# Attention unit 2's turn moved behind head 0's queries, unit 5's probabilities in another buffer, mix(1,a,1) ahead of tile 1's attention

## The reference

```python
proj = rms_norm(x) @ w_in                                  # u, v, q, k, v
a_out = gelu(u) * (w_s @ rms_norm(gelu(v)) + b_s)          # per block of 128 tokens, 8 groups
b_out = banded_chunk_attention(q, k, v)                    # 8 heads of 64, softmax
x = x + concat(a_out, b_out) @ w_out
q = rms_norm(x) @ w_query                                  # 8 routing heads, 2 x 128
s_top, i_top = top_k(q @ sub_keys, 16)                     # per half
best, pos = top_k(s_top[0][:, None] + s_top[1][None, :], 16)
eidx = i_top[0] * 128 + i_top[1]                           # at pos
h = gelu(expert_u[eidx] . x)
x = x + sum(softmax(best) * h * expert_v[eidx])            # 16384 experts, 16 a head and token
```

## Time and profile before

| | us |
|---|---|
| median of three runs | 1156.43 |
| the profiled execution, its own time | 1155.34 |
| its span | 1153.5 |
| TensorE matmuls busy | 1048.9 (91%) |
| VectorE busy | 769.7 (67%) |
| ScalarE busy | 568.4 (49%) |
| GpSimd busy | 289.4 (25%) |
| DMA, mean over the span | 322 GB/s |

### The profile page before, as it was taken

The page is one execution under the profiler, slowest core; times in us unless marked ns, Lnnn a source line. Parts: engine busy times, 40 slices in busy tenths (PEclk is TensorE's granted clock), DMA queues, the critical chain, the costliest instruction groups (busy, mean ns, idle before and its releaser), DMA issues.

```text
span 1153.5 us, 12038 instructions
## 1 busy us (share of the span) xinstructions
PE 1048.9 (91%) x4092; PEld 667.5 (58%) x4092; DVE 769.7 (67%) x1499; ACT 568.4 (49%) x1237; POOL 289.4 (25%) x261
## 2 busy tenths in 40 slices
PE   8999999998898779799877887789999999999998
PEld 6888464454454333344322232259878778888886
DVE  5788777667666657676676665554675496777743
ACT  7664544544443444643444345354765555444532
POOL 0001445444535325453443444400000000000000
PEclk9999999999999989999999999999999999999999
DMA  9848999999999999999999999977443454555540
GB/s 349 341 167 304 421 422 422 421 421 422 420 421 422 421 422 421 422 421 420 422 422 421 422 411 422 421 291 269 177 146 131 163 186 161 183 187 191 196 156 36
DMA packets 55532, 371.87 MB, mean 322 GB/s; under 512 B 6192, under 2 KB 7344, under 8 KB 12080
## 3 DMA queue, kind: packets, MB, share of 16 engines
q0 software_dynamic: 36864, 268.45, 56.0%
q1 hardware_dynamic: 18608, 102.65, 24.2%
HBM read 370.03 MB, written 1.05 MB: 322 GB/s over the span
## 4 chain that ended last, share of the span: by engine, by line
PE 53%; DMA 31%; DVE 7%; ACT 6%; issue 3%; POOL 0%; SPq 0%; DVEq 0%; POOLq 0%; ACTq 0%
DMA uv<-in_peer_uv,eidx 30%; PE bank L2269 14%; PE bank L1968 7%; PE bank L1970 7%; PE bank L1969 7%; PE bank L2445 6%; PE bank L2040 4%; PE bank L2444 3%; DVE uv L1581 3%; DVE w_lo L1290 1%; ACT w_hi L806 1%; ACT diag L1026 1%; PE bank L1939 1%; ACT chosen L1023 1%; PE bank L2158 1%
## 5 line engine op out<-in xcount | busy, mean ns | idle before, releaser
L2269 PE MATMUL bank<-uv,diag 128*128 128x512 f32 x1024 | 490.8, 614 | 90.9 <-ACT diag L1026 90.6
L1581 DVE SCALAR_TENSOR_TENSOR uv<-uv,xn 128x1024 f32<-128x1024 f32 x256 | 313.7, 1225 | 209.6 <-DMA uv<-in_peer_uv,eidx 209.5
L730 POOL DMA_INDIRECT uv<-in_peer_uv,eidx x256 | 289.1, 1129 | 457.3 <-PE bank L2269 329.3
L2269 PEld LDWEIGHTS bank<-uv,diag 128*128 128x128 f32 x1024 | 184.3, 193 | 362.1 <-issue 359.9
L1290 DVE TENSOR_TENSOR w_lo<-wraw,w_hi 128x2048 fp32r<-128x2048 f32 x69 | 157.7, 2290 | 94.7 <-ACT w_hi L806 94.7
L1018 ACT ACTIVATE chosen<-chosen 128x1 f32<-128x1 f32 x256 | 51.8, 202 | 327.7 <-DVE uv L1581 327.2
L806 ACT CAST w_hi<-wraw 128x2048 fp32r<-128x2048 f32 x69 | 131.6, 1909 | 124.2 <-PE bank L1970 62.1
L2445 PE MATMUL bank<-nT_both,w_hi 128*128 128x512 f32 x320 | 109.6, 396 | 0.0
L1026 ACT ACTIVATE diag<-const,chosen 128x128 f32<-128x128 f32 x256 | 102.8, 401 | 8.3
L1023 ACT ACTIVATE chosen<-chosen 128x1 f32<-128x1 f32 x256 | 75.4, 295 | 9.3
L2444 PE MATMUL bank<-nT_both,w_lo 128*128 128x256 f32 x280 | 78.1, 279 | 0.0
(11 more groups left out here) (326 smaller groups left out, 1363.4 us busy)
## 6 DMA issues: line engine op xcount, KB each, us to landing
wraw<-in_ff_in SPq DMA_DIRECT2D x22, 1024.0 KB, 4.7
wraw<-in_ff_out SPq DMA_DIRECT2D x11, 1024.0 KB, 4.7
wraw<-in_query SPq DMA_DIRECT2D x4, 1024.0 KB, 5.0
uv<-in_peer_uv,eidx POOLq DMA_INDIRECT x256, 15.0
wraw<-in_in_q SPq DMA_DIRECT2D x2, 1024.0 KB, 8.3
wraw<-in_in_k SPq DMA_DIRECT2D x2, 1024.0 KB, 9.0
wraw<-in_pool_o SPq DMA_DIRECT2D x2, 1024.0 KB, 4.7
wraw<-in_sb_o SPq DMA_DIRECT2D x2, 1024.0 KB, 4.6
```

The source lines that it names most:

```text
L730: pool.indirect_dma_start(out=uv[:, RING_AT[n % RING], :], out_offset=None, in_=io["peer_uv"], in_offset=bass.IndirectOffsetOnAxis(ap=eidx ...
L1581: nc.vector.scalar_tensor_tensor(out=u, in0=u, scalar=1.0, in1=xn[:, head // PEER_HEADS, :], op0=ALU.mult, op1=ALU.mult, accum_out=hdot[he ...
L2269: mm = nc.tensor.matmul(acc[m][:, :], diag[:, n % RING, :], uv[:, RING_AT[n % RING], D + m * HALF:D + (m + 1) * HALF], start=(n % (ROWS // ...
```

## The change

Five things are changed. Unit 2 is turned behind head 0's queries, where unit 3 was turned, and its copy on ScalarE goes behind head 0's route. Unit 3 is turned behind mix(1,a,1). mix(1,a,1) goes from behind the attention of tile 1 to directly behind mix(0,a,1). Unit 5's probabilities lie in `u_sb` of tile 0, which is free once turn_gmlp(0) has read it, so that slot 2 of `prob` can keep unit 2's for longer. In the decoding, the row and column of a place are written side by side, so that one cast in place of two makes them floats. The list of banks follows.

```diff
+    use("pT", 2)
+    use("route0")
+    for n in range(2):
+        held.add(use("w_out", n, 1))
     use("pT", 3)
-    use("route0")
-    held.add(use("w_out", 0, 1))
     held.add(use("oT", 1))
     use("pT", 4)
     use("pT", 5)
-    held.add(use("w_out", 1, 1))
...
+        def prob_of(u):
+
+            return u_sb[:, 0, :] if u == len(UNITS) - 1 else prob[:, u % 3, :]
...
             exps(3)
-            copy_pT(2)
             exps(4)
...
             router_scores(0, (0,))
-            for u in (3, 4, 5):
+            for u in (2, 3, 4, 5):
                 copy_pT(u)
...
-                if u >= 3:
+                if u in (3, 4):
 
                     wait_full(dve, "pT", u - 3)
+                elif u == 5:
+                    wait_full(dve, "aT", 0)
...
                 elif part == 1:
-                    nc.vector.tensor_copy(ij[:, first:last], rank[:, 3, to])
-                    later(nc.vector.tensor_copy(ij[:, TOPK + first:TOPK + last], cols16[:, to]))
+                    later(nc.vector.tensor_copy(two(ij)[:, :, to], places[:, :, to]))
...
-                nc.vector.tensor_copy(ij[:, 0:8], rank[:, 3, 0:8])
-                step(nc.vector.tensor_copy(ij[:, TOPK:TOPK + 8], cols16[:, 0:8]))
+                step(nc.vector.tensor_copy(two(ij)[:, :, 0:8], places[:, :, 0:8]))
...
             mix(0, "a", 0, True)
-            turn_prob(2)
             scores(5)
             spatial(1)
...
             query_0(1, 1)
-            turn_prob(3)
+            turn_prob(2)
             pe.wait_ge(subk_loaded, 16)
             wait_read(pe, "query0", 0)
             router_scores(0, (0,))
             wait_read(pe, "aT", 1)
             mix(0, "a", 1, True)
+            mix(1, "a", 1, True)
+            turn_prob(3)
             heads_out(2)
             turn_prob(4)
             heads_out(3)
             turn_prob(5)
             heads_out(4)
             heads_out(5)
-            mix(1, "a", 1, True)
             wait_read(pe, "oT", 1)
```

More of the change, by code:

```diff
@@ L182, in psum_uses @@
     held.remove(uses["proj", 0, 1][0])
-    use("pT", 2)
     use("score", 5)
@@ L322, in two_block_kernel @@
         small = sb("small", [P, 256])
-        rank = sb("rank", [P, 4, TOPK], U32)
+        rank = sb("rank", [P, 3, TOPK], U32)
         eidx = sb("eidx", [P, DEEP, TOPK], U32)
@@ L457, in two_block_kernel @@
         iota = small[:, 240:256]
-        cols16 = small[:, 144:160].bitcast(U32)
+        places = small[:, 144:176].bitcast(U32).rearrange("p (a b) -> p a b", a=2)
         unread = small[:, 229:240]
+        def prob_of(u):
+            return u_sb[:, 0, :] if u == len(UNITS) - 1 else prob[:, u % 3, :]
         bank_full = [sem(f"bank_full{b}") for b in range(8)]
@@ L906, in exps @@
                 for a in range(heads):
-                    ins = nc.scalar.activation(prob[:, u % 3, a * w:(a + 1) * w], prob[:, u % 3, a * w:(a + 1) * w], ACT.Exp,
+                    part = prob_of(u)[:, a * w:(a + 1) * w]
+                    ins = nc.scalar.activation(part, part, ACT.Exp,
                                                bias=attn_stat[:, 1, u, a:a + 1], accum_out=attn_stat[:, 2, u, a:a + 1])
@@ L1408, in maxima @@
                 src = wait_full(dve, "score", u)
-                if u >= 3:
+                if u in (3, 4):
                     wait_full(dve, "pT", u - 3)
+                elif u == 5:
+                    wait_full(dve, "aT", 0)
                 t, heads = UNITS[u][0], len(UNITS[u][1])
                 first = BIAS_HEADS.index(UNITS[u][1][0])
-                p3d = prob[:, u % 3, :].rearrange("p (a b) -> p a b", a=heads)
+                p3d = prob_of(u).rearrange("p (a b) -> p a b", a=heads)
                 nc.vector.tensor_tensor(p3d, src[:, :].rearrange("p (a b) -> p a b", a=heads),
@@ L1557, in decode @@
                 if part == 0:
-                    nc.vector.tensor_scalar(rank[:, 3, to], rank[:, 2, to], 4, None, ALU.logical_shift_right)
-                    later(nc.vector.tensor_scalar(cols16[:, to], rank[:, 2, to], 15, None, ALU.bitwise_and))
+                    nc.vector.tensor_scalar(places[:, 0, to], rank[:, 2, to], 4, None, ALU.logical_shift_right)
+                    later(nc.vector.tensor_scalar(places[:, 1, to], rank[:, 2, to], 15, None, ALU.bitwise_and))
                 elif part == 1:
-                    nc.vector.tensor_copy(ij[:, first:last], rank[:, 3, to])
-                    later(nc.vector.tensor_copy(ij[:, TOPK + first:TOPK + last], cols16[:, to]))
+                    later(nc.vector.tensor_copy(two(ij)[:, :, to], places[:, :, to]))
                 elif part == 2:
@@ L1624, in eight_best @@
                 step(nc.vector.max_index(rank[:, 2, 0:8], b[:, 0:8], corner))
-                nc.vector.tensor_scalar(rank[:, 3, 0:8], rank[:, 2, 0:8], 3, None, ALU.logical_shift_right)
-                step(nc.vector.tensor_scalar(cols16[:, 0:8], rank[:, 2, 0:8], 7, None, ALU.bitwise_and))
-                nc.vector.tensor_copy(ij[:, 0:8], rank[:, 3, 0:8])
-                step(nc.vector.tensor_copy(ij[:, TOPK:TOPK + 8], cols16[:, 0:8]))
+                nc.vector.tensor_scalar(places[:, 0, 0:8], rank[:, 2, 0:8], 3, None, ALU.logical_shift_right)
+                step(nc.vector.tensor_scalar(places[:, 1, 0:8], rank[:, 2, 0:8], 7, None, ALU.bitwise_and))
+                step(nc.vector.tensor_copy(two(ij)[:, :, 0:8], places[:, :, 0:8]))
                 hits = onehot[:, :, 0:8, 0:8]
@@ L2100, in turn_prob @@
                 pe.wait_ge(prob_ready, u + 1)
-                transposes(prob[:, u % 3, :], "pT", u)
+                transposes(prob_of(u), "pT", u)
             def heads_out(u):
```

## The result

The changed kernel takes 1159.76 us (median of 8 runs, 1158.39 to 1162.38) beside 1156.28 for the kernel before (8 runs, 1155.36 to 1157.93): ratio 1.0032, 95% interval 1.0023 to 1.0040. It is slower by 3.5 us, where no change had been forecast (1155.9, range 1154.2 to 1157.9).

What follows compares the result with a forecast made beforehand. The DMA stream of gathered rows, near 422 GB/s for some 640 us, was taken as the bound. Turn -0.44, decoding -0.06, early gathers 0 and absorbed lateness 0 gave -0.5 us: 1155.9 against the 1156.43 median, range 1154.2 to 1157.9.

Steps and rivals of the forecast that it cites:

- Part 1: Ahead of the gathers: moved unit turn saves 0.44 us and merged decoding cast 0.06; gather 0 issued 0.5 us earlier.
- Part 2: mix(1,a,1) ahead of the attention: gather 2 goes 4.7 us earlier, but only the queue's order changes; worth 0.
- A: Rival at the stream's start: early gathers close the thin stretch too, -1.35 us in all, 1155.1; chance 0.15.
- C: Rival at the stream's start: early gathers recover all 2.9 us of dead time in 102.5:113.5, 1153.5; chance 0.04.
- Part 3: Before mix(0,b,1): rounding and remainder lose their cover, TensorE idles 1.42 us, gather 4 and later work about 1.4 late.
- Part 4: SP's three loads behind heads_out(5): 2.9 us later, there by 122.4, first used by TensorE at 133.7; hidden.
- Does the lateness reach the stream?: At gathers 4 and 28: demand 1.9 us against spares of 3.5 and 2.9, so lateness is absorbed, 0.
- Part 5: Unit 5's probabilities, slot 2 and bank order: newly shared banks last read over a microsecond before opening; costs nothing.
- sign of a cause behind 760 us: Sign of being wrong: stream at the same rate but the end moved by more than 2 us.
- B: Slower rival: new TensorE idle brings a second clock dip, 1156.5 mild (chance 0.10), 1159.4 in full (0.05).
- no real spare: At the gather queue, the slower rival's full form: 5.7 us not to be had, all 3.0 us pass through; chance 0.05.
- second dip of the clock: After TensorE's new idle: granted clock 0.5 behind 110 while the dip at 127 stays; lateness 3.5 us at gather 28.

Runs made afterwards that it cites:

- a_mixback_rank4: Changed kernel with `rank` at four rows and mix(1,a,1) back behind heads_out(5), banks with it: 1155.24 us, ratio 0.9991 to the kernel before.
- a_rot_hold: a_rank4_rot with gathers 2 and 3 held until heads_out(5) is over: 1156.55 us, ratio 1.0005 to the kernel before.
- a_rank4: Changed kernel with `rank` at its old four rows, buffers behind it at old addresses: 1157.48 us, ratio 1.0010 to the kernel before.
- b_rank3: Kernel before with only the shorter `rank` (three rows, row 3 put into `small`), no cast merged: 1158.68 us, ratio 1.0022.
- a_rank4_rot: a_rank4 with the list of banks turned by seven ahead of y_x: 1156.35 us, ratio 1.0007 to the kernel before.
- m_late: a_mixback_rank4 with useless TensorE products ahead of mix(0,b,1), making gather 4 2.9 us later: 1157.19 us, ratio 1.0006 to the kernel before.
- rot_swap: a_rank4_rot with mix(1,b,1) before mix(0,b,1), so gather 4 goes earlier: 1156.62 us, ratio 0.9999 to the kernel before.
- b_at75520: Kernel before with `xstat` behind the ring and padding, ring starting at byte 75520: 1147.08 us, ratio 0.9924.
- b_at75552: Kernel before with `xstat` behind the ring and padding, ring starting at byte 75552 as in the change: 1158.45 us, ratio 1.0018.

## Why the prediction was wrong

| step | predicted | shown |
|---|---|---|
| unit turns and decoding | -0.5 | -0.8 (a_mixback_rank4) |
| gathers 2 and 3 early | 0 | 0 within the scatter (a_rot_hold) |
| the uncovered wait | 0, absorbed | +1.1 by medians |
| the list of banks | 0 | +0.9 by medians, 1.06 in the trace |
| 64 bytes less in `rank` | not costed | +2.3 (a_rank4) to +2.6 (b_rank3) |
| sum | -0.5 | +3.5 |

**Part 1** held. Gather 0 is issued 83.5 us behind the 61st matmul, before 84.1: 0.6 earlier, 0.5 forecast. The merged cast stands alone, 0.17 us:
```profile
100.73 0.17 DVE L1632 CAST small<-small 128x16 f32<-128x16 uint32 x1
```
**Part 2** held in its sum. Gather 2 follows gather 0 by 2.64 us (2.6 forecast), and a_rot_hold and a_rank4_rot move the same 366 GB/s in 35 us. Rivals A and C fell with it: neither a rate near 400 in all of 105 to 119 nor an earlier stream came.

**Part 3** held as to what happens, to a tenth: idle 1.47 us for 1.42, gather 4 14.35 us behind gather 0 for 14.3. **Part 4** held: counted from the 61st matmul the pieces go 2.7 us later (2.9 forecast), and TensorE takes the first at 136.14, behind other work and without idle time.

**"Does the lateness reach the stream?"** is the step that failed first. I took gather 4's 9.2 us to landing, less the 5.7 of a gather in an idle queue, as 3.5 us of spare. But landing is when the last byte is there, and the engines thin out before that. In before, the first packet of gather 4 followed its issue by 4.8 us, in after by 2.6, of which GpSimd itself works 1.90; that is the shortest seen at this place. So there were some 2.2 us of spare in front of its first byte, not 3.5. Even they would have held the 1.9 us of demand, and the first packet of row 4 is not late (100.5 us behind the 61st matmul, before 101.3).

The loss lies behind it, where the prediction had nothing: in after row 5 starts 3.3 us behind row 4, and row 6 3.0 behind row 5, in place of 2.49. The packets of rows 4 and 5 took 370 and 360 ns in the mean, single ones over 1.2 us, those of rows 10 to 255 315; in before rows 4 and 5 took 310. Gather 5 had been issued by then (118.99, the first packet of row 4 comes at 119.40), so it isn't for want of a follower. The packets of row 0, which also come to a queue without gathers, take 379. Why they are slow stays open. Measured from a_mixback_rank4, a lateness of 1.5 us (a_rank4_rot) cost 1.0 in row 10, and one of 2.9 (m_late) cost 2.2, each from one trace with the scatter named above; the spare that the prediction counted on is not there. The Trainium skill (DMA: Bandwidth & Descriptors, Anatomy of one DMA), by whose 4.4 us (an estimate) the spare would have been larger still, leads further away; the lowest landing recorded for gather 4 is 6.4 us (m_late), for gather 0 5.5, so the trace doesn't agree.

**Part 5** failed in "each bank that is newly shared was last read over a microsecond before it is opened". I followed the banks through the stage at hand and into the gathers, but the list goes on to the end of block 2, and 800 us behind the edit y_x(0,0) met a bank that was read 0.8 us too late. Of the 1.06 us by which the stretch is longer, 0.8 are this wait. The prediction's sign of a cause behind 760 us was an end that moves at an unchanged rate; the rate did change, and of the 3.5 us in the medians only this 1 us lies there.

**What had no step at all** is the largest: shortening `rank` was read as a saving of memory, and the sum has no term for it. That it moves the ring, into which all 268 MB of rows are written, I did not ask. The full stream sets the pace for 620 us, so 0.3% on its rate is 2 us, more than every wait that the change adds or removes.

The rivals: B, the one on the slower side, had 1159.4 in its full form, close to the result by luck: two thirds of the loss are the ring's place, which it doesn't have. Its "no real spare" is nearly right; its second dip of the clock did not come (1.00 in 109:112). The Trainium skill (TensorE: Matmul & The Clock Gate, What's actually happening), which makes the clock depend on how busy the engine has lately been, had been named beside it; an idle time of 1.47 us in this stretch did not bring the clock down. In m_late and rot_swap even the old dip is absent from the 35 us (mean granted clock 1.00 against 0.95), and m_late is slow all the same: the dip is not what costs.

## What to carry to other kernels

Where a DMA stream sets the pace, the address of the buffer that it fills is part of the design: look at what an edit to any array ahead of it does to that address, and try a few starts (here 75520, a multiple of 256, was worth 9 us, more than any reordering in this case). A spare in a queue is measured at the first byte of the late transfer, not at the landing of its last byte, and the distance of the transfers behind it has to be looked at too: here the first was not late against the kernel before, and those behind it were. And a list that gives out banks or buffers in turn carries a local edit to the far end of the kernel; compare each stage's duration, not only the one that was edited.

## What the runs showed of the hardware

**The start of the target.** Gathers of 8192 bytes a partition stream at 427 GB/s into a ring that starts at a multiple of 256 bytes, at 419 when it starts 32 bytes to either side of it, and at 421 at the four starts 64 to 160 bytes above. The Trainium skill (DMA: Bandwidth & Descriptors, How a descriptor splits into AXI transactions) says that a transfer is cut into pieces at multiples of 256 bytes, and that one which starts off such a multiple needs an extra, partly used piece. It speaks of what is read; here the written side was moved. The trace agrees that the multiple of 256 is the fastest: by the rule 8192 bytes are 32 pieces or 33, 3.1% as an estimate, and 1.3 to 1.6% are measured. It does not agree on the rest: the page's waste grows with the remainder, by its beats of 32 bytes from 0.4% at 32 to 2.7% at 224 as an estimate, while 32 and 224 are both 2.493 us and 64 to 160 are faster than either. Why is open, and so is whether other multiples of 256 do as well, since only 75520 was tried. A kernel that joins that start with the reordering of a_mixback_rank4 wasn't run; b_at75520, at 1147.08, is the fastest here and beats both kernels.

Nor does the start act by itself. In every trace more than half of the packets of rows 0 to 3 take 309 ns, wherever the ring starts; the longer ones set in later, with row 5 in b_at75552 and only with row 10 in after, which has the same start and whose rows 7 to 10 still come 2.45 us apart. In b_at75520 they never set in. What sets them in was not tried.

**Scatter.** Executions of one kernel differ by 1 us in start-up and by the stretches at half clock. These come to 16 to 38 us in sum over the execution in the profiles taken, and they do not go with the time: before has 29 us of them and took 1155.34, its repeat 16 and took 1156.17.
